# Gate projections inside an unrolled attention pipeline, and value products on 64 columns

## The chip, the core and the metric

One core of a Trainium2 chip. The time is the device time of one execution in microseconds (us); median of 3 runs before: 3261.18 (3258.07 to 3262.68). Engines: TensorE (PE: matmuls, and its weight loads, PEld), VectorE (DVE), ScalarE (ACT), GpSimd (POOL), SyncE (SP), which issues the DMAs.

## The reference

Two transformer blocks over one sequence of 512 tokens, 1024 wide, in float32. The change touches the mixer of the first:

```python
xn = rmsnorm(h, ln_mix_g[l])
z = xn @ w_in[l] + b_in[l]
q, k, v, pz, ga, gp = jnp.split(z, SPLITS, axis=-1)
y_a = sliding_window_attention(q, k, v, attn_sinks[l]) @ w_attn_up[l]
y_p = multiscale_pool(pz, w_pool_grp[l], pool_scale[l]) @ w_pool_up[l]
merged = jax.nn.sigmoid(ga) * y_a + jax.nn.sigmoid(gp) * y_p
h = h + merged @ w_o[l]
```

Attention has 16 query heads of 64 in two groups, each group with one key and value head. A block of 128 queries sees its own 128 keys and the 128 before them, and a sink value per head joins the softmax. The pool branch takes sliding means over 2, 4, 8 and 16 tokens. After this mixer come a product-key expert layer, a second mixer (RWKV and GLA scans) and a feed-forward layer; they make up most of the time.

## The kernel before

Activations lie with channels on the partitions: a tile is 128 channels by 512 tokens, and 1024 channels are 8 tiles.

**The weight stream.** All dense weights pass in one order through `Dense`, in slots of 128 x 1024 (512 KB), one for each output tile. To keep the precision of float32, a slot is split into a rounded high part and a low remainder: SP loads it raw (`load`, L141), ACT copies the high part (`high`, L150), POOL subtracts it for the low part (`low`, L158), and PE makes 24 matmuls of 512 columns of it, three for each of 8 input tiles (`product`, L256 to L258). Two slots can be raw and two split. `high` of a slot waits until PE has used the slot two before it (`used`), `low` waits for `high`, and a load waits for the split of the slot two before. Outputs go round over four PSUM banks, each given back (`free`) by the engine that reads it. Every engine has its own order of instructions, written out in the kernel, and waits for the others by semaphores.

**First mixer** (`first_mixer`), in three blocks with all engines joined between them:

1. *Projections*, 31 slots: 8 for queries, 8 for each of the two gates (sigmoid on the way out, L576), 4 for the pool input, 2 for keys, 1 for values. Values are wanted by token, so this slot's products take the activations as stationary operand: 96 matmuls of 128 columns, read out by DVE (L608).
2. *Attention* (`attention`), a loop over 4 blocks of 128 tokens. DVE first stages the block's queries and values (L829, L831). Then 8 steps of two heads each: score products (L792), DVE scales, masks and takes the maximum (L837 to L844), ACT exponentials (L873, L875), DVE normalises (L851 to L855), PE transposes (L805), ACT copies them (L882), PE value products (L816), ACT output (L886). PE issues the scores of two steps ahead between the transposes and the value products of a step. The value products of both heads add up in one output of 128 rows, with values padded with zeros in the half of the other head. POOL does the sliding sums of the pool branch meanwhile (L772 to L781). No weight slot is used in this block.
3. *Merge*, 20 slots: the pool groups' products (L722), 8 slots for the attention output, 4 for the pool branch, 8 for the output product. ACT first rounds the attention output (L383), then scales the four pool groups (L671), then makes high copies; DVE splits (L389, L691), then multiplies each result with its gate (L695, L699), which frees the bank.

Of the kernel before, what the change touches and what calls it, by code (L numbers as in the profile page):

```python
# [400 lines left out]
def layout_params(a):  # L401

    def col(v):
# [15 lines left out]
        ("b_v", np.broadcast_to(b[qw + kw:o_pool][None, :], (P, kw))),  # L419
# [38 lines left out]
def layout_constants():  # L458
# [22 lines left out]
    parts = [("mask", np.concatenate([mask0, mask, mask, mask], 1)), ("inv_count", inv), ("ident", ident),  # L481
# [27 lines left out]
def first_mixer(nc, k, dram):  # L509

    dense, norm, par, h, ps, consts = k.dense, k.norm, k.par, k.h, k.ps, k.consts
    with ExitStack() as ctx:
# [10 lines left out]
        vals = sb("values_by_token", [P, NB + 1, NKV * HD])  # L523
        yp = sb("pooled", [P, len(PW), T])
        cm = sb("mask_by_block", [P, NB, 2 * P])
# [4 lines left out]
        zeroed = sem("pool_engine_zeroed")  # L530
        x_in = [sem(f"x_loaded{n}") for n in range(4)]

        with nc.Block() as block:
            @block.sync
            def _(sp):
# [7 lines left out]
                sp.dma_start(cm[:, :, :], dram["consts"][:, 0:NB * 2 * P].rearrange("p (b n) -> p b n", b=NB)).then_inc(k.boot, 16)  # L543
                sp.dma_start(gw[:, :, :], dram["w_group"]).then_inc(k.boot, 16)
                w.run(sp, w.load, 7, BANK)
                w.run(sp, w.load, 1, 3)

            @block.gpsimd
            def _(pool):
                w = dense.cursor()  # L550
                pool.memset(keys[:, :, :, :], 0.0).then_inc(zeroed, 1)
                pool.memset(vals[:, 0, :], 0.0).then_inc(zeroed, 1)
                pool.memset(zp[:, :, 0:16], 0.0).then_inc(zeroed, 1)
                dense.low_first(pool)
                w.run(pool, w.low, 7, BANK)
                w.run(pool, w.low, 1, 3)

            @block.scalar
            def _(act):
# [21 lines left out]
                gemm_out(lambda m: ga[:, m, :], par("b_ga"), ACT.Sigmoid)  # L581
                gemm_out(lambda m: gp[:, m, :], par("b_gp"), ACT.Sigmoid)
# [27 lines left out]

            @block.tensor
            def _(pe):
# [4 lines left out]
                w.multiply(pe, 7, lambda t: chunk(xn, t), [DC], lambda t: norm.ready(pe, t))  # L617
                for v in range(NKV):
# [15 lines left out]
        dense.close(31, 32)  # L634
        ctx_xn.close()

        attention(nc, k, q, keys, vals, cm, zp, yp)
# [6 lines left out]
        group_done, group_out, group_split, rounded, split, merged, added = (sem(n) for n in (  # L644
            "pool_group_product", "pool_group_scaled", "pool_group_split", "merge_high", "merge_low", "gates_merged",
            "residual_added"))
        G = len(PW)
        with nc.Block() as block:
# [15 lines left out]
            def _(act):  # L664
# [20 lines left out]
            def _(dve):  # L685
# [11 lines left out]
                for m in range(DC):  # L697
                    dve.wait_ge(dense.used, w.slots + m // 2 + 1)
# [33 lines left out]
def attention(nc, k, q, keys, vals, masks, zp, yp):  # L732


    ps, par, consts = k.ps, k.par, k.consts
    with ExitStack() as ctx:
        def sb(name, shape, dt=F32):
# [4 lines left out]
        qs = sb("query_block", [P, QC, P])  # L742
        vs = sb("value_blocks", [P, 2, NKV, 2, P])
# [3 lines left out]
        mx, nm, su, es, den, rc = (sb(n, [P, NH]) for n in (  # L747
            "row_max", "negated_max", "row_sum", "sink_exp", "denominator", "reciprocal"))
        nsink = sb("negated_sinks", [P, NH])
        inv = sb("inverse_counts", [P, len(PW), T])  # L750
        w1, w2 = (sb(n, [P, len(PW), 16 + T]) for n in ("window_sums_a", "window_sums_b"))
        inv_in, zeroed, staged, scored, scaled, chain, negmax, exps, probs, turned, copied, mixed, out, pooled = (
            sem(n) for n in ("inverse_counts_loaded", "value_blocks_zeroed", "query_block_staged", "scores_product",
                             "scores_scaled", "attention_vector_chain", "negated_max_ready", "exps_done", "probs_ready",
                             "probs_transposed", "transposed_copied", "value_product", "attention_out", "pool_chain"))
        with nc.Block() as block:
            @block.sync
            def _(sp):
                sp.dma_start(inv[:, :, :], k.dram["inv_count"]).then_inc(inv_in, 16)
                sp.wait_ge(k.boot, 64)  # L760

            @block.gpsimd
            def _(pool):
                pool.memset(vs[:, :, :, :, :], 0.0).then_inc(zeroed, 1)
# [3 lines left out]
                src = zp  # L768
                for n, dst in enumerate((w1, w2, w1, w2)):
                    lag = PW[n] // 2  # L770
                    pool.wait_ge(pooled, 2 + n)
                    pool.tensor_tensor(dst[:, n:, 16:], src[:, n:, 16:], src[:, n:, 16 - lag:16 + T - lag],  # L772
                                       ALU.add).then_inc(pooled, 1)
                    src = dst
                pool.wait_ge(pooled, 6)
                pool.wait_ge(inv_in, 16)
                for g in range(len(PW)):
                    pool.tensor_tensor(yp[:, g, :], (w1, w2)[g % 2][:, g, 16:], inv[:, g, :], ALU.mult).then_inc(pooled, 1)
                for g in range(len(PW)):
                    pool.wait_ge(pooled, 7 + g)  # L780
                    pool.tensor_tensor(yp[:, g, :], yp[:, g, :], zp[:, g, 16:], ALU.subtract).then_inc(pooled, 1)  # L781

            @block.tensor
            def _(pe):
                with pe.Fori(0, NB) as b:
                    pe.wait_ge(staged, b * 3 + 3)

                    def scores(c):
                        if c >= 2:
                            pe.wait_ge(scaled, b * QC + (c - 1))  # L790
                        for half in range(2):
                            mm = pe.matmul(ps[:, c % 2, half * 2 * P:(half + 1) * 2 * P], qs[:, c, :],  # L792
                                           keys[:, c * NKV // QC, half, bass.ds(b * P, 2 * P)], start=True, stop=True)
                        mm.then_inc(scored, 1)

                    scores(0)
                    scores(1)
                    for c in range(QC):
                        pe.wait_ge(probs, b * QC + (c + 1))
                        if c:  # L800
                            pe.wait_ge(copied, b * QC + c)
                        for half in range(2):
                            for kb in range(2):
                                n = half * 2 + kb
                                mm = pe.transpose(ps[:, 2, n * P:(n + 1) * P], e[:, c % 2, half, kb * P:(kb + 1) * P],  # L805
# [2047 lines left out]
```

## Time and profile before

| | us |
|---|---|
| median of 3 runs | 3261.18 |
| profiled execution, its span (no other time of it is shown) | 3257.4 |
| PE busy | 2995.8 (92%) |
| DVE busy | 1793.6 (55%) |
| POOL busy | 1265.8 (39%) |
| ACT busy | 1068.2 (33%) |
| projections, from the first weight product to the value slot | 34.1 to 198.96 |
| attention block | 214.1 to 388.7 |

Busy times overlap between the engines. A PE record lasts longer than its share of PE's time, since matmuls are pipelined: the distance of starts counts.

### The profile page before, as it was taken

The numbers are of one execution on the slowest core, as the hardware profiler recorded it, in microseconds if no ns is written. First come the engines' busy times: TensorE is split into PE (matmuls) and PEld (weight loads), VectorE is DVE, ScalarE is ACT, GpSimd is POOL, SyncE is SP. The second block draws the span as 40 slices with busy tenths as digits, with TensorE's granted clock in tenths as the row PEclk, the third lists the DMA queues.
The fourth block names the chain that finished last, engine by engine and source line by source line (L and its number), as shares of the span: only waits on it lengthen the run. The fifth ranks groups of instructions, "written<-read, shape, count | busy, mean of one in ns | idle before, by whom it ended". The sixth has DMA issues, their size and how long they took to land. (4 is left out here: it accounts for less than half of the span.)

```text
span 3257.4 us, 52236 instructions
## 1 busy us (share of the span) xinstructions
PE 2995.8 (92%) x19808; PEld 2486.5 (76%) x19808; DVE 1793.6 (55%) x2626; ACT 1068.2 (33%) x1656; POOL 1265.8 (39%) x634
## 2 busy tenths in 40 slices
PE   7976698999999999999999999979869978899997
PEld 5864577888888888878888888856669966588775
DVE  1025426987477777427777777762836554433115
ACT  3324423333333333321111111134422335433323
POOL 3450033355444444444444444433332222244442
PEclk8988899999999999999999999989989989999998
DMA  3320022344445545565555555522652101233331
GB/s 119 97 71 0 7 85 90 92 141 141 126 163 205 175 159 174 211 185 190 197 196 196 196 190 190 184 91 78 205 150 52 36 15 39 65 96 96 98 104 65
DMA packets 173617, 404.59 MB, mean 124 GB/s; under 512 B 55216, under 2 KB 55344, under 8 KB 172208
## 3 DMA queue, kind: packets, MB, share of 16 engines
q1 hardware_dynamic: 173488, 402.72, 39.1%
q8 instruction: 100, 1.64, 0.2%
q14 instruction: 29, 0.24, 0.0%
HBM read 318.77 MB, written 83.89 MB: 124 GB/s over the span
## 5 line engine op out<-in xcount | busy, mean ns | idle before, releaser
L158 POOL TENSOR_TENSOR weights_low<-weights_raw,weights_high 128x1024 fp32r<-128x1024 f32 x435 | 1129.9, 2598 | 1686.6 <-ACT weights_high L150 1686.6
L150 ACT ACTIVATE weights_high<-weights_raw 128x1024 fp32r<-128x1024 f32 x435 | 461.0, 1060 | 1694.8 <-PE psum L258 1677.6
L256 PE MATMUL psum<-expert_in_high,weights_high 128*128 128x512 f32 x1152 | 458.4, 398 | 8.9 <-DVE expert_in_low L351 4.3
L257 PE MATMUL psum<-expert_in_low,weights_high 128*128 128x512 f32 x1152 | 449.7, 390 | 0.0
L258 PE MATMUL psum<-expert_in_high,weights_low 128*128 128x512 f32 x1152 | 449.6, 390 | 0.0
L256 PE MATMUL psum<-coefficients_high,weights_high 128*128 128x512 f32 x1024 | 399.6, 390 | 5.9 <-DVE coefficients_low L1172 4.2
L257 PE MATMUL psum<-coefficients_low,weights_high 128*128 128x512 f32 x1024 | 399.3, 390 | 0.0
L258 PE MATMUL psum<-coefficients_high,weights_low 128*128 128x512 f32 x1024 | 399.1, 390 | 0.0
L1172 DVE TENSOR_TENSOR coefficients_low<-activation_in,coefficients_high 128x512 fp32r<-128x512 f32 x128 | 354.8, 2772 | 4.4
L256 PEld LDWEIGHTS psum<-expert_in_high,weights_high 128*128 128x128 f32 x1152 | 217.1, 188 | 57.3 <-issue 10.2
L258 PEld LDWEIGHTS psum<-expert_in_high,weights_low 128*128 128x128 f32 x1152 | 216.8, 188 | 45.6
L257 PEld LDWEIGHTS psum<-expert_in_low,weights_high 128*128 128x128 f32 x1152 | 217.2, 189 | 41.3
L1153 DVE TENSOR_TENSOR second_key_weighted<-st_and_second_key_onehot,choices 128x512 f32<-128x512 f32 x128 | 225.7, 1763 | 19.4 <-DVE st_and_second_key_onehot L1149 2.2
L1169 DVE TENSOR_TENSOR coefficients_high<-activation_in,table_group 128x512 fp32r<-128x512 f32 x128 | 88.6, 692 | 264.6 <-PE psum L258 264.6
L256 PEld LDWEIGHTS psum<-coefficients_high,weights_high 128*128 128x128 f32 x1024 | 192.8, 188 | 46.7 <-DVE coefficients_low L1172 4.6
L258 PEld LDWEIGHTS psum<-coefficients_high,weights_low 128*128 128x128 f32 x1024 | 192.8, 188 | 40.2
L257 PEld LDWEIGHTS psum<-coefficients_low,weights_high 128*128 128x128 f32 x1024 | 192.8, 188 | 40.1
L1149 DVE TENSOR_TENSOR st_and_second_key_onehot<-tables,choices 128x1024 f32<-128x1024 f32 x128 | 157.1, 1227 | 115.1 <-PE psum L1050 100.5
L256 PE MATMUL psum<-mix_in_high,weights_high 128*128 128x512 f32 x464 | 187.3, 404 | 33.4 <-POOL weights_low L113 14.8
L257 PE MATMUL psum<-mix_in_low,weights_high 128*128 128x512 f32 x464 | 182.4, 393 | 0.0
L258 PE MATMUL psum<-mix_in_high,weights_low 128*128 128x512 f32 x464 | 182.2, 393 | 0.0
L256 PE MATMUL psum<-ffn_in_high,weights_high 128*128 128x512 f32 x352 | 138.3, 393 | 4.8 <-DVE ffn_in_low L351 4.8
(390 smaller groups left out, 4786.1 us busy)
## 6 DMA issues: line engine op xcount, KB each, us to landing
weights_raw<-in_weights SPq DMA_DIRECT2D x437, 512.0 KB, 3.6
expert_activations<-expert_activation SPq DMA_DIRECT2D x128, 256.0 KB, 4.2
coefficient_table<-table_stage SPq DMA_DIRECT2D x8, 4096.0 KB, 13.6
table_group<-coefficient_table SPq DMA_DIRECT2D x128, 256.0 KB, 4.1
activation_in<-expert_activations SPq DMA_DIRECT2D x128, 256.0 KB, 3.7
chunk_vectors<-scan_vectors SPq DMA_DIRECT2D x8, 1280.0 KB, 8.4
scan_vectors<-scan_stage SPq DMA_DIRECT2D x4, 1280.0 KB, 6.7
scan_vectors<-scan_stage SPq DMA_DIRECT2D x4, 1024.0 KB, 6.0
```

Of the source, the lines that this page charges most:

```text
L150: act.activation(d.hi[:, m % SPLIT, :], d.raw[:, m % RAW, :], ACT.Copy).then_inc(d.high, 1)
L158: pool.tensor_tensor(d.lo[:, m % SPLIT, :], d.raw[:, m % RAW, :], d.hi[:, m % SPLIT, :].bitcast(F32), ALU.subtract).then_inc(d.split, 1)
L256: pe.matmul(acc, w[0][:, cols], x[0], start=start, stop=False)
L257: pe.matmul(acc, w[0][:, cols], x[1], start=False, stop=False)
L258: return pe.matmul(acc, w[1][:, cols], x[0], start=False, stop=stop)
L1149: dve.tensor_tensor(onehot[:, u, :, :, :], iota[:, None, None, :].to_broadcast([P, 2, QT, NK]), sel[:, 0:2, bass.ds(t, QT)][:, :, :, None] ...
L1153: dve.tensor_tensor(second[:, u, :, :], onehot[:, u, 1, :, :], sel[:, 2, bass.ds(t, QT)][:, :, None].to_broadcast([P, QT, NK]), ALU.mult). ...
L1169: dve.tensor_tensor(by_block(co[0][:, o, :]), by_block(tile), gt, ALU.mult).then_inc(ex.part, 1)
L1172: dve.tensor_tensor(co[1][:, o, :], tile, co[0][:, o, :].bitcast(F32), ALU.subtract).then_inc(ex.coef, 1)
```

## The change

The gates' 16 slots move from the projections into the attention block, and with them their place in the weight stream. The loop over blocks is unrolled into 32 steps. In each, PE does 12 of the gates' 24 matmuls per slot between the scores of two steps ahead and the value products; ACT reads the gates out after each second step, without the sigmoid, which ACT applies in the merge. Queries, keys and values are no longer staged per block. The value slot has the usual form; its result by channel is transposed by PE and copied by DVE twice, once for each half. Attention's banks are 4 to 7. The value products of each head have 64 columns of the array and 64 output rows, in turn by head.

Core of the diff ("..." where lines are left out; DVE's and the score products' lines in attention change in their indices only, `q` and `keys` being read in place):

```diff
-        vals = sb("values_by_token", [P, NB + 1, NKV * HD])
+        vals = sb("values_by_token", [P, NB + 1, NKV, 2, P])
...
-                w.run(sp, w.load, 7, BANK)
+                w.run(sp, w.load, 3, BANK)
...
                 gemm_out(lambda m: q[:, m, :], par("b_q"), ACT.Identity)
-                gemm_out(lambda m: ga[:, m, :], par("b_ga"), ACT.Sigmoid)
-                gemm_out(lambda m: gp[:, m, :], par("b_gp"), ACT.Sigmoid)
...
                 w.high(act, 0, NKV, 3)
+                w.full_wait(act, 0, NKV)
+                act.activation(vt[:, :], dense.acc[NKV], ACT.Identity, bias=par("b_v")).then_inc(dense.free[NKV], 1)
                 act.sem_inc(dense.free[3], 1)
...
-                w = dense.cursor()
-                w.advance(7 * BANK)
-                w.full_wait(dve, 0, 2)
-                dve.tensor_tensor(vals[:, 1:, :], dense.acc[2].rearrange("p (b n) -> p b n", b=NB),
-                                  par("b_v")[:, None, :].to_broadcast([P, NB, P]), ALU.add).then_inc(dense.free[2], 1)
+                dve.wait_ge(zeroed, 3)
+                dve.wait_ge(turned, 1)
+                for half in range(2):
+                    dve.tensor_copy(vals[:, 1:, :, half, half * HD:(half + 1) * HD],
+                                    ps[:, 5, :].rearrange("p (b v n) -> p b v n", b=NB, v=NKV))
...
-                w.multiply(pe, 7, lambda t: chunk(xn, t), [DC], lambda t: norm.ready(pe, t))
-                for v in range(NKV):
+                w.multiply(pe, 3, lambda t: chunk(xn, t), [DC], lambda t: norm.ready(pe, t))
+                for v in range(NKV + 1):
...
-                w.free_wait(pe, 0, 2)
-                w.slot_wait(pe, 0, 2, 3)
-                wv = w.weights(2)
+                pe.wait_ge(dense.free[NKV], w.units // BANK + 2)
                 for b in range(NB):
-                    cols = slice(b * P, (b + 1) * P)
-                    for t in range(DC):
-                        x, y = chunk(xn, t, cols), (wv[0][:, t * P:(t + 1) * P], wv[1][:, t * P:(t + 1) * P])
-                        mm = product(pe, dense.acc[2][:, cols], x, 0, y, t == 0, t == DC - 1)
-                mm.then_inc(dense.used, 1)
+                    mm = pe.transpose(ps[:, 5, b * P:(b + 1) * P], vt[:, b * P:(b + 1) * P], consts("ident"))
+                mm.then_inc(turned, 1)
         norm.close(squares=DC, roots=1, splits=1)
...
-                for g in range(G):
-                    act.wait_ge(group_done, g + 1)
-                    for dst in (yps, ypp[0]):
-                        ins = act.activation(dst[:, g, :], ps[:, 4 + g, :], ACT.Copy, scale=par("pool_scale")[:, g:g + 1])
-                    ins.then_inc(group_out, 1)
-                w.run(act, w.high, 2, BANK)
+
+                def gate(x, m):
+                    act.activation(x[:, m, :], x[:, m, :], ACT.Sigmoid).then_inc(gated, 1)
+
+                for m in range(DC):
+                    gate(ga, m)
+                for j in range(DC):
+                    w.high(act, 0, j, DC)
+                    if j < G:
+                        act.wait_ge(group_done, j + 1)
+                        for dst in (yps, ypp[0]):
+                            ins = act.activation(dst[:, j, :], ps[:, 4 + j, :], ACT.Copy, scale=par("pool_scale")[:, j:j + 1])
+                        ins.then_inc(group_out, 1)
+                    gate(gp, j)
+                w.advance(DC)
...
+                    dve.wait_ge(gated, m + 1)
...
+    STEPS, GATES = NB * QC, 2 * DC
+    PART = DC * GATES // STEPS
+    TURNED, OUT = 6, 7
...
+        inv = gp[:, 0:len(PW), :]
...
+                w = dense.cursor()
+                for j in range(GATES):
+                    w.load(sp, 0, j, GATES)
...
+                w.low(pool, 0, 0, GATES)
...
+                w.low(pool, 0, 1, GATES)
...
+                for j in range(2, GATES):
+                    w.low(pool, 0, j, GATES)
...
+                def gate_part(n):
+                    j, first = n * PART // DC, n * PART % DC
+                    if first == 0:
+                        w.free_wait(pe, j // BANK, j % BANK)
+                        w.slot_wait(pe, 0, j, GATES)
+                    for t in range(first, first + PART):
+                        mm = product(pe, dense.acc[j % BANK], w.weights(j), t, chunk(xn, t), t == 0, t == DC - 1)
+                    if first + PART == DC:
+                        mm.then_inc(dense.used, 1)
+
+                scores(0)
+                scores(1)
+                for n in range(STEPS):
+                    b, kv = n // QC, n % QC * NKV // QC
+                    pe.wait_ge(probs, n + 1)
+                    if n:
+                        pe.wait_ge(copied, n)
+                    for half in range(2):
+                        for kb in range(2):
+                            at = half * 2 + kb
+                            mm = pe.transpose(ps[:, TURNED, at * P:(at + 1) * P], e[:, n % 2, half, kb * P:(kb + 1) * P],
+                                              consts("ident"))
+                    mm.then_inc(turned, 1)
+                    if n + 2 < STEPS:
+                        scores(n + 2)
+                    gate_part(n)
+                    pe.wait_ge(copied, n + 1)
+                    if n:
+                        pe.wait_ge(out, n)
...
+                    for kb in range(2):
                         for half in range(2):
+                            at = half * 2 + kb
+                            mm = pe.matmul(ps[rows(half), OUT, 0:P], vals[:, b + kb, kv, half, rows(half)],
+                                           pt[:, at * P:(at + 1) * P], start=(kb == 0), stop=(kb == 1))
+                    mm.then_inc(mixed, 1)
...
+                def gate_out(j):
+                    dst, bias = (ga, par("b_ga")) if j < DC else (gp, par("b_gp"))
+                    if j == DC:
+                        act.wait_ge(pooled, 6 + len(PW))
+                    w.high(act, 0, j, GATES)
+                    w.full_wait(act, j // BANK, j % BANK)
+                    act.activation(dst[:, j % DC, :], dense.acc[j % BANK], ACT.Identity,
+                                   bias=bias[:, j % DC:j % DC + 1]).then_inc(dense.free[j % BANK], 1)
+
+                exp(0)
+                exp(1)
+                for n in range(STEPS):
+                    act.wait_ge(turned, n + 1)
+                    act.activation(pt[:, :], ps[:, TURNED, :], ACT.Copy).then_inc(copied, 1)
+                    if n + 2 < STEPS:
+                        exp(n + 2)
+                    if (n + 1) * PART % DC == 0:
+                        gate_out((n + 1) * PART // DC - 1)
+                    act.wait_ge(mixed, n + 1)
+                    act.activation(q[:, n % QC, block_of(n)], ps[:, OUT, 0:P], ACT.Copy).then_inc(out, 1)
+        dense.close(GATES, GATES)
...
-    w_z = np.concatenate([w_in[:, 0:qw], w_in[:, o_ga:], w_in[:, o_pool:o_ga], wk[0], wk[0], wk[1], wk[1],
-                          w_in[:, qw + kw:o_pool]], 1)
+    w_z = np.concatenate([w_in[:, 0:qw], w_in[:, o_pool:o_ga], wk[0], wk[0], wk[1], wk[1], w_in[:, qw + kw:o_pool],
+                          w_in[:, o_ga:]], 1)
```

## Rows read from the trace of the kernel before

**Rows 1.** The page: PE's line of busy time, and the clock in 40 slices.

```profile
PE 2995.8 (92%) x19808; PEld 2486.5 (76%) x19808; DVE 1793.6 (55%) x2626; ACT 1068.2 (33%) x1656; POOL 1265.8 (39%) x634
...
PEclk8988899999999999999999999989989989999998
```

**Rows 2.** Stretches: us, busy (instructions) by engine, clock, DMA share, GB/s; projections, attention.

```profile
34.10:198.96 164.86, 164.86 (x720) 136.28 (x719) 0.00 (x0) 53.47 (x63) 71.09 (x30) 0.99 0.32 101
...
214.10:388.70 174.60, 103.41 (x512) 82.92 (x512) 92.42 (x205) 77.11 (x260) 22.04 (x15) 0.80 0.03 9
```

**Rows 3.** Instructions of L576: duration min/median/max ns, first and last start.

```profile
L576 ACT ACTIVATE q_then_attention_out<-psum,params x8: 668/668/668, 42.4 to 80.5; 128x512 f32 x8
...
L576 ACT ACTIVATE gate_pool<-psum,params x8: 668/668/668, 129.4 to 167.5; 128x512 f32 x8
L576 ACT ACT_TABLE_LOAD  x2: 1283/1283/1283, 86.0 to 107.8; - x2
```

**Rows 4.** Timeline, value slot to attention: start, duration, engine, line, operation, [idle before].

```profile
198.96 0.22 PE L256 MATMUL psum<-weights_high,mix_in_high 128*128 128x128 f32 x1
...
209.83 0.69 DVE L608 TENSOR_TENSOR values_by_token<-psum,params 128x512 f32<-128x512 f32 x1 [179.08 <-PE psum L258]
...
211.02 2.34 POOL L158 TENSOR_TENSOR weights_low<-weights_raw,weights_high 128x1024 fp32r<-128x1024 f32 x1 [8.29 <-ACT weights_high L150]
...
214.12 0.33 SPq L759 DMA_DIRECT2D inverse_counts<-in_consts  x1
```

**Rows 5.** Timeline, the start of attention.

```profile
215.94 3.89 DVE L831 COPY value_blocks<-values_by_token 128x256 f32 x2
...
219.98 3.78 PE L792 MATMUL psum<-keys_by_kv_and_half,query_block 128*128 x8 [10.19 <-DVE value_blocks L831]
...
228.92 1.11 PE L805 MATMUL psum<-tables,probabilities 128*128 128x128 f32 x4 [5.16 <-DVE probabilities L855]
```

**Rows 6.** Timeline, a settled attention step.

```profile
245.22 0.66 PE L805 MATMUL psum<-tables,probabilities 128*128 128x128 f32 x4 [1.75 <-DVE probabilities L855]
...
245.72 1.03 PE L792 MATMUL psum<-keys_by_kv_and_half,query_block 128*128 x4
...
246.58 1.14 PE L816 MATMUL psum<-probabilities_transposed,value_blocks 128*128 128x128 f32 x8
246.78 0.69 DVE L837 SCALAR_TENSOR_TENSOR scores<-psum,mask_by_block 128x512 f32<-128x512 f32 x1 [1.62 <-PE psum L792]
...
248.42 0.51 ACT L873 ACTIVATE probabilities<-scores,negated_max 128x256 f32<-128x256 f32 x1 [1.91 <-DVE negated_max L844]
...
248.72 0.69 DVE L855 TENSOR_TENSOR probabilities<-probabilities,reciprocal 128x512 f32<-128x512 f32 x1
...
249.47 0.66 PE L805 MATMUL psum<-tables,probabilities 128*128 128x128 f32 x4 [1.74 <-DVE probabilities L855]
```

**Rows 7.** Timeline, DVE with POOL at work beside it.

```profile
231.17 5.39 POOL L781 TENSOR_TENSOR pooled<-pooled,pool_in 128x512 f32<-128x512 f32 x4
...
231.78 0.69 DVE L837 SCALAR_TENSOR_TENSOR scores<-psum,mask_by_block 128x512 f32<-128x512 f32 x1 [2.92 <-PE psum L792]
...
233.99 1.45 DVE L855 TENSOR_TENSOR probabilities<-probabilities,reciprocal 128x512 f32<-128x512 f32 x1
```

**Rows 8.** Timeline of PE in the second mixer's scan: 32 small records.

```profile
2504.63 1.15 PE L2007 MATMUL psum<-X_transposed,L_level_times_X 64*64 64x64 f32 x32
```

**Rows 9.** Timeline, the start of the merge.

```profile
388.78 4.27 ACT L383 ACTIVATE ion_out_then_merged_high<-q_then_attention_out 128x512 fp32r<-128x512 f32 x8 [0.54 <-PEq L756]
...
397.70 0.69 DVE L691 TENSOR_TENSOR pool_groups_split_low<-pool_in,pool_groups_split_high 128x512 fp32r<-128x512 f32 x1 [0.47 <-ACT pool_groups_split_high L671]
...
403.44 1.06 ACT L150 ACTIVATE weights_high<-weights_raw 128x1024 fp32r<-128x1024 f32 x1 [4.38 <-PE psum L258]
```

**Rows 10.** Timeline, PE's first matmul after an idle gap.

```profile
463.45 0.76 PE L256 MATMUL psum<-ion_out_then_merged_high,weights_high 128*128 128x512 f32 x1 [5.65 <-DVE tion_out_then_merged_low L389]
```

**Rows 11.** The stretch behind that gap, columns as in rows 2.

```profile
464.00:468.00 4.00, 4.00 (x11) 3.03 (x10) 4.00 (x7) 2.28 (x4) 0.00 (x0) 0.50 0.04 15
```

More of the change, by code:

```diff
@@ L551, in _ @@
                 pool.memset(keys[:, :, :, :], 0.0).then_inc(zeroed, 1)
-                pool.memset(vals[:, 0, :], 0.0).then_inc(zeroed, 1)
+                pool.memset(vals[:, :, :, :, :], 0.0).then_inc(zeroed, 1)
                 pool.memset(zp[:, :, 0:16], 0.0).then_inc(zeroed, 1)
                 dense.low_first(pool)
-                w.run(pool, w.low, 7, BANK)
+                w.run(pool, w.low, 3, BANK)
                 w.run(pool, w.low, 1, 3)
@@ L697, in _ @@
                 for m in range(DC):
+                    dve.wait_ge(gated, DC + m + 1)
                     dve.wait_ge(dense.used, w.slots + m // 2 + 1)
@@ L746, in attention, with score_bank, rows, block_of @@
         pt = sb("probabilities_transposed", [P, 4 * P])
-        mx, nm, su, es, den, rc = (sb(n, [P, NH]) for n in (
+        mx, nm, su, es, den, rc = (sb(n, [P, 2 * STEPS]) for n in (
             "row_max", "negated_max", "row_sum", "sink_exp", "denominator", "reciprocal"))
         nsink = sb("negated_sinks", [P, NH])
[L750 to L755, printed above, removed]
+        inv = gp[:, 0:len(PW), :]
+        w1, w2 = (sb(n, [P, len(PW) - at, 16 + T]) for at, n in enumerate(("window_sums_a", "window_sums_b")))
+        inv_in, scored, scaled, chain, negmax, exps, probs, turned, copied, mixed, out, pooled = (
+            sem(n) for n in ("inverse_counts_loaded", "scores_product", "scores_scaled", "attention_vector_chain",
+                             "negated_max_ready", "exps_done", "probs_ready", "probs_transposed", "transposed_copied",
+                             "value_product", "attention_out", "pool_chain"))
+        def score_bank(n):
+            return ps[:, 4 + n % 2, :]
+        def rows(half):
+            return slice(half * HD, (half + 1) * HD)
+        def block_of(n):
+            return slice(n // QC * P, (n // QC + 1) * P)
         with nc.Block() as block:
@@ L781, in _ @@
                     pool.tensor_tensor(yp[:, g, :], yp[:, g, :], zp[:, g, 16:], ALU.subtract).then_inc(pooled, 1)
+                for j in range(2, GATES):
+                    w.low(pool, 0, j, GATES)
             @block.tensor
             def _(pe):
[L785 to L790, printed above, removed]
-                        for half in range(2):
[L792 to L805, printed above, removed]
-                                                  consts("ident"))
-                        mm.then_inc(turned, 1)
-                        if c + 2 < QC:
-                            scores(c + 2)
-                        pe.wait_ge(copied, b * QC + (c + 1))
-                        if c:
-                            pe.wait_ge(out, b * QC + c)
-                        for half in range(2):
-                            for kb in range(2):
-                                n = half * 2 + kb
-                                mm = pe.matmul(ps[:, 3, 0:P], vs[:, kb, c * NKV // QC, half, :], pt[:, n * P:(n + 1) * P],
-                                               start=(n == 0), stop=(n == 3))
-                        mm.then_inc(mixed, 1)
-                    pe.wait_ge(out, b * QC + QC)
@@ new lines, in _, with scores @@
+                w = dense.cursor()
+                def scores(n):
+                    c = n % QC
+                    if n >= 2:
+                        pe.wait_ge(scaled, n - 1)
+                    for half in range(2):
+                        mm = pe.matmul(score_bank(n)[:, half * 2 * P:(half + 1) * 2 * P], q[:, c, block_of(n)],
+                                       keys[:, c * NKV // QC, half, n // QC * P:n // QC * P + 2 * P], start=True, stop=True)
+                    mm.then_inc(scored, 1)
@@ new lines, in _, with scale_and_max @@
+                link = Count(chain, 1)
+                def scale_and_max(n):
+                    r, h = slice(2 * n, 2 * n + 2), slice(n % QC * 2, n % QC * 2 + 2)
+                    dve.wait_ge(scored, n + 1)
+                    dve.scalar_tensor_tensor(
+                        out=s[:, n % 2, :, :], in0=score_bank(n).rearrange("p (g n) -> p g n", g=2), scalar=SCALE,
+                        in1=masks[:, int(n >= QC):int(n >= QC) + 1, :].to_broadcast([P, 2, 2 * P]),
+                        op0=ALU.mult, op1=ALU.add).then_inc(scaled, 1)
+                    dve.wait_ge(scaled, n + 1)
+                    link.inc(dve.tensor_reduce(mx[:, r], s[:, n % 2, :, :], AXX, ALU.max))
+                    link.wait(dve)
+                    dve.scalar_tensor_tensor(out=nm[:, r], in0=mx[:, r], scalar=-1.0, in1=nsink[:, h],
+                                             op0=ALU.mult, op1=ALU.min).then_inc(negmax, 1)
@@ new lines, in normalise @@
+                def normalise(n):
+                    r = slice(2 * n, 2 * n + 2)
+                    dve.wait_ge(exps, 4 * (n + 1))
+                    link.inc(dve.tensor_tensor(den[:, r], su[:, r], es[:, r], ALU.add))
+                    link.wait(dve)
+                    link.inc(dve.reciprocal(rc[:, r], den[:, r]))
+                    link.wait(dve)
+                    dve.tensor_tensor(e[:, n % 2, :, :], e[:, n % 2, :, :],
+                                      rc[:, r, None].to_broadcast([P, 2, 2 * P]), ALU.mult).then_inc(probs, 1)
@@ new lines, in _, with exp @@
+                w = dense.cursor()
+                def exp(n):
+                    act.wait_ge(negmax, n + 1)
+                    for half in range(2):
+                        j, head = 2 * n + half, n % QC * 2 + half
+                        act.activation(e[:, n % 2, half, :], s[:, n % 2, half, :], ACT.Exp, bias=nm[:, j:j + 1],
+                                       accum_out=su[:, j:j + 1]).then_inc(exps, 1)
+                        act.activation(es[:, j:j + 1], par("sinks")[:, head:head + 1], ACT.Exp,
+                                       bias=nm[:, j:j + 1]).then_inc(exps, 1)
```

98 lines of the change are left out of this document (25 added, 73 removed).

## The prediction

> **What bounds the kernel now.** I read the page first. TensorE (PE) is busy 92% of the span, and the granted clock is lower than elsewhere in the first slice and in slices 3 to 5, 163 to 407 us [rows 1]. The change touches only the first mixer, so I cut that into stages. The input projection is a solid block of PE work: 164.86 us busy out of 164.86 at clock 0.99. The attention is not: in 174.60 us PE is busy 103.41, VectorE (DVE) 92.42, ScalarE (ACT) 77.11, nothing is loaded, and the clock averages 0.80 [rows 2]. So the first stage is bound by PE, the second by a chain of small steps.
>
> That chain is one attention step (two heads of one block), 32 in all. In a settled step the transposes start at 245.22 and the next ones at 249.47: 4.25 us. In between PE issues transposes (0.50 us to the start of the scores), scores (0.86 to the start of the value products) and value products; DVE takes the scores at 246.78 and ends the normalising multiply at 248.72 + 0.69 = 249.41; the transposes follow [rows 6]. The eight value records have 128 moving columns each and the four score records 256, 1,024 in both, so the value products take the same 0.86 to issue. PE therefore works 0.50 + 0.86 + 0.86 = 2.22 us of 4.25 and waits for DVE in the rest. Four blocks have 8 x 4.25 = 34 us of this each, 136 in all; the other 38 us are starts and ends of blocks, where the clock is low.
>
> **Part 1, the projection loses 16 weight slots.** The last query output starts at 80.5 and the last gate output, 16 slots later, at 167.5: 87.0 us, 5.44 a slot [rows 3]. ACT's, GpSimd's (POOL) and SP's share of these slots lies beside PE, so exactly PE's time goes: -87.0.
>
> The value slot changes form. Before, its 96 short matmuls run from 198.96 to 209.8 [rows 4]; now it has 24 matmuls of 512 columns like every slot, 5.44: -5.4. Its end gets longer. Before, the last split (0.2 handoff, 1.06 high, then low until 213.36) ended the stage and attention began at 214.12, 4.3 after PE. Now, behind the same high copy, come one 0.67 activation, four transposes (0.66), two DVE copies of 512 elements (0.69 each, taking the price of a row that reads as much), four handoffs of about 0.1, then the same 0.7 for the change of block: 5.1, so +0.8. If DVE's copies are held up by POOL's split it is 0.7 more. Sum: -91.6; attention starts at about 122.5.
>
> **Part 2, the start of attention.** Staging of queries and values is gone; it held the first scores until 219.98, mostly two DVE copies of 3.89 us behind POOL's window sums [rows 5]. That is 5.9 us after 214.12; now 0.3. From first scores to first transposes it is 8.9 us, at half clock with the window sums alongside; this stays. First transposes: 122.5 + 0.3 + 8.9 = 131.7.
>
> **Part 3, the loop.** Each step gets 12 of the gates' matmuls, half a slot: 2.72. They stand behind the scores of two steps ahead and in front of the value products. The DVE chain starts at the scores, so it is not lengthened: probabilities are ready 4.25 after the step's start as before. PE's own work becomes 2.22 + 2.72 = 4.94, more than 4.25. PE becomes the bound, with 0.7 us of margin per step for everybody else. I checked the others by laying an odd step (the one that ends a slot) out from 0, with these durations: exponentials 3.2 to 4.65, gates' last matmul done 4.4, high copy 4.65 to 5.7, gate output to 6.4, attention output of this step to 6.65, transposed copy of the next step to 7.3; the value products of the next step are issued at 9.0. ACT has 1.7 to spare. POOL's low split (2.4) runs 5.75 to 8.15; SP's loads of 512 KB fit many times over. The next slot's weights are needed only three steps later.
>
> The value products: four matmuls of 64 columns of the array, in alternation between the halves. Moving columns are as many as before. Bounds: the scans' products on a quarter of the array with 64 moving columns issue 32 records in 1.15 us, tail included, some 29 ns each [rows 8]. At the pace of the score records (0.86 / 1,024 columns) a record of 64 columns takes 54, so there two quarters run side by side. Those differ in rows and in columns, our halves in columns only. If ours ran side by side, a step would lose 0.43: 4.51. On the other side a record of 128 columns lasts 0.27 us and more against 0.11 of issue, so a pipe emptied at a seam costs about 0.17; at four seams a step that is 0.68: 5.62. I take 5.1, near the plain count, with one seam.
>
> The Trainium skill (TensorEngine Tiling (Array Packing), Key Properties) says that changing the tiling mode drains TensorE. No row here goes between the 64-column and the full form in a dense stretch, so the trace doesn't decide it; by the rule there are two such changes per step, 0.34, and the step would be 5.28, 6 us more in all. The skill (TensorE: Matmul & The Clock Gate, Part 3, What overlaps and what doesn't) also has weight loads overlap only where the row group differs, which speaks against the gain of 0.43; the scan's rows fit it, as their halves do differ in rows.
>
> 32 x 5.1 = 163.2. The last two steps issue no scores: -1.7. At the start the clock is at half: after an idle spell it was for 4.8 us of dense work [rows 10, 11], which loses 2.4. In the first steps POOL also has window products and differences to do: with POOL at work a DVE multiply of two SBUF operands took 1.45 rather than 0.69, the scaling that reads PSUM stayed at 0.69 [rows 7]; this lengthens some five chains by about 1, of which the margin takes 0.7: +1. Sum 164.9; PE ends at 296.6. The block then ends not with PE but with the last split for the merge: the gates' last matmul is about 0.6 before PE's end, then high 1.06, low 2.4, 0.7 for the block: 300.2. Before: 388.8. So -88.6 to here; attention itself takes 177.7 against 174.6.
>
> **Part 4, the merge gets the sigmoids.** ACT rounds eight tiles in 4.27 [rows 9], then loads a table (1.28, [rows 3]) and does eight sigmoids at 0.67: 10.9 after the merge's start. Only then comes the high copy that slot 2 needs; with the low copy it is done at 14.4, just when PE has used slots 0 and 1 (ACT took slot 1's release at 403.44, 14.7 after the start). No loss. But the pool groups' output number j is now behind the high copy of slot j, which waits until slot j was used, and DVE multiplies no gate before it has split all four groups. Group 3: slot 3 used at 25.5, high to 26.6, two activations to 27.9, split 28.6, product 29.3. PE needs that bank for unit 4 at 25.3: +4.1. Before, the groups were split by 398.4, in slot 1.
>
> Two idle gaps are new: 3.5 us ahead of the merge and these 4.1. After a gap of 5.65 PE ran at half clock for 4.8 [rows 10, 11], a loss of 2.4; I take half of that for each gap, +2.4. Sum of the merge: +6.5.
>
> **Sum.** -91.6 + 3.1 + 6.5 = -82.0. Nothing later is edited. The profiled execution shows only its span, 3257.4; with the change 3175.4. The median of the runs shown is 3.8 above that span, and I carry this over: 3261.2 - 82.0 = 3179.
>
> **Rivals.**
> (a) POOL takes DVE's place in the loop. Each slot's low split (2.4) could fall on the normalising multiply, which then waits for it [rows 7]. For: 16 splits are new here. Against: by the layout they fall in the even step's PSUM-reading scaling, and end before its multiply. Price: 4.25 + 2.4 = 6.65 in one step of two instead of 5.1: 16 x 1.55 = +25, 3204.
> (b) Better than forecast: halves side by side, and no loss of clock in the merge: 32 x 0.59 = 19 less, but never under the chain's 4.25: 3158 to 3165.
> (c) The chains don't overlap: a wait puts the gates' matmuls between scores and DVE or delays the transposes by them, and a step is 4.25 + 2.72 = 6.97. +60: 3239. Against: scores stand ahead of the gates on PE, and their semaphore is on the score product itself.
> (d) Slower than before: the clock stays at half in the mixed loop. A step then is 9.9, +154, 3333. It decides against the change from (5.1 + 82 / 32 =) 7.7 us per step, that is, with the clock at half in over half of the loop. For: attention's average of 0.80. Against: the low clock there goes with idle starts of blocks, and steps in which PE was idle for 1.7 of 4.25 us ran at full clock [rows 6]; now PE never pauses. The skill's TensorE page (Part 4) says that transposes don't count as busy in the same way; here they are a tenth of PE's time, and no row isolates it.
>
> **Chances.** Forecast 0.72 (3162 to 3200: step 4.6 to 5.6, merge +3 to +10), (a) 0.12, (b) 0.09, (c) 0.04, (d) 0.03. A measurement of this kernel tells about 0.2%, 6.5 us, from no change; only (d) and unforeseen losses end there or beyond it: faster 0.95, same 0.01, slower 0.04. Range 3162 to 3205.
>
> **What would show it.** Right: projection ends near 118, first transposes near 132, 32 steps of 5.0 to 5.2 in which PE waits for nothing, merge from about 300, one PE wait of 4 us on DVE's gate product after slot 3. Wrong: PE waiting for the multiply in the loop (a), value products at half their issue time (b), steps near 7 (c), granted clock 0.5 after the first steps (d).

## The result and the profile after

| | before | after |
|---|---|---|
| median, us | 3260.64 (4 runs) | 3169.96 (4 runs, 3168.03 to 3171.49) |
| ratio | | 0.9718, 95% interval 0.9704 to 0.9732 |
| span of the profiled execution | 3257.4 | 3166.7 |

The change saves 90.7 us; 82 were forecast, and the time lies in the range given (3162 to 3205). In the page of the kernel after, PE's line and the clock [rows 1] read:

```profile
PE 2960.5 (93%) x19740; PEld 2449.9 (77%) x19740; DVE 1794.3 (57%) x2615; ACT 1066.7 (34%) x1666; POOL 1265.6 (40%) x633
...
PEclk9999999999999999999999999989899988999998
```

The dip of the clock in slices 3 to 5 is gone. The kernel's stretches (columns as [rows 2]) are the projections, the start of attention, and the loop from its second step to just before its end:

```profile
34.10:112.00 77.90, 77.90 (x341) 64.33 (x340) 0.00 (x0) 23.04 (x29) 32.03 (x14) 0.99 0.33 108
...
120.50:129.87 9.37, 2.92 (x8) 1.89 (x9) 7.95 (x10) 2.93 (x12) 8.98 (x6) 0.55 0.48 168
...
137.00:284.00 147.00, 145.99 (x855) 114.08 (x852) 78.04 (x177) 88.83 (x266) 46.86 (x23) 1.00 0.17 54
```

PE is busy 145.99 of 147.00 us in the loop; in the attention block before it was busy 103.41 of 174.60 [rows 2]. The timeline of one step, against [rows 6], with the gates' matmuls left out:

```profile
137.15 0.66 PE L840 MATMUL psum<-tables,probabilities 128*128 128x128 f32 x4
...
137.64 1.03 PE L816 MATMUL psum<-keys_by_kv_and_half,q_then_attention_out 128*128 128x256 f32 x4
...
138.71 0.69 DVE L865 SCALAR_TENSOR_TENSOR scores<-psum,mask_first_and_other 128x512 f32<-128x512 f32 x1 [3.38 <-PE psum L816]
...
140.62 0.69 DVE L882 TENSOR_TENSOR probabilities<-probabilities,reciprocal 128x512 f32<-128x512 f32 x1
...
141.36 0.66 PE L852 MATMUL psum<-probabilities_transposed,values_by_token 128*64 128x128 f32 x8
...
141.95 0.66 PE L840 MATMUL psum<-tables,probabilities 128*128 128x128 f32 x4
```

The probabilities are ready at 140.62 + 0.69 = 141.31; PE comes for them at 141.95 and doesn't wait. The step is 4.79 (4.79 to 4.81 in 27 of the 31 distances between transposes; the first, at half clock, is 7.28), and the value products take 0.59 of it. The merge is where time was given back. Its first instructions, PE's wait after slot 3, and the stretch behind that wait:

```profile
288.86 4.28 ACT L383 ACTIVATE ion_out_then_merged_high<-q_then_attention_out 128x512 fp32r<-128x512 f32 x8 [2.46 <-PEq L774]
288.88 5.28 PE L729 MATMUL psum<-pooled,pool_group_weights 128*128 128x512 f32 x8 [3.79 <-PEq L774]
...
318.31 1.78 DVE L696 TENSOR_TENSOR pool_groups_split_low<-pool_in,pool_groups_split_high 128x512 fp32r<-128x512 f32 x1 [3.59 <-ACT pool_groups_split_high L675]
320.01 2.47 DVE L701 TENSOR_TENSOR gate_attention<-psum,gate_attention 128x512 f32<-128x512 f32 x4
```

```profile
320.93 0.76 PE L256 MATMUL psum<-ion_out_then_merged_high,weights_high 128*128 128x512 f32 x1 [4.97 <-DVE gate_attention L701]
```

```profile
320.93:326.19 5.26, 5.26 (x13) 4.09 (x13) 1.55 (x3) 0.00 (x0) 0.00 (x0) 0.50 0.23 93
```

In the kernel before, the pool groups' products, the first row of PE in the merge, ran at full clock:

```profile
388.80 3.67 PE L722 MATMUL psum<-pooled,pool_group_weights 128*128 128x512 f32 x8 [0.96 <-PEq L756]
```

| mark in the timeline, us | before | forecast | after |
|---|---|---|---|
| attention starts | 214.1 | 122.5 | 120.6 |
| first transposes | 228.9 | 131.7 | 129.9 |
| a settled step | 4.25 | 5.1 | 4.79 |
| merge starts | 388.8 | 300.2 | 288.9 |
| first product with the expert keys, after the merge | 535.5 | 453.5 | 445.0 |

The lead is 99.9 us at the merge's start and 90.5 behind it.

### The profile page after: what moved, and what is told of

The parts are those of the page before. It is cut to its first block and busy times, and to the rows that moved or that the text cites. A ratio compares the mean times of both kernels' runs of the same rounds, so it can differ in the third digit from the quotient of the medians.

```text
span 3166.7 us, 51665 instructions
## 1 busy us (share of the span) xinstructions
PE 2960.5 (93%) x19740; PEld 2449.9 (77%) x19740; DVE 1794.3 (57%) x2615; ACT 1066.7 (34%) x1666; POOL 1265.6 (40%) x633
## 5 line engine op out<-in xcount | busy, mean ns | idle before, releaser
L256 PE MATMUL psum<-mix_in_high,weights_high 128*128 128x512 f32 x472 | 196.3, 416 | 33.2 <-POOL weights_low L113 14.8
```

The source lines that it names most:

```text
L256: pe.matmul(acc, w[0][:, cols], x[0], start=start, stop=False)
```

## The experiments

All times but one are medians of several executions, measured beside the kernel before, whose own median was 3258.3 to 3262.8 on these occasions. A step is the distance from one step's transposes to the next one's; a settled step is one away from the start and the end of the loop.

**Where the 91 us come from.** The first leaves the unrolled attention and puts the gates back in the projections, with the sigmoid there and the merge as before; the loop keeps everything but the gates' matmuls, with their loads, splits and read-outs:

```diff
-                    gate_part(n)
```

> One part alone: the unrolled attention, the new value slot and the 64-column products, but the gates' 16 slots back in the projections with their sigmoid, and the merge as before. Theory (the gain is mostly the overlap): attention is 9.3 to its first transposes and 32 x 4.25 from there, some 146 in place of 174.7; projections 4.5 less than before; merge as before: 3260.6 - 29 - 4.5 = 3227. So 57 of the 91 us come from the overlap. Rival (unrolling and the staging that goes make most of it): 3200 or less.

3249.7, ratio 0.9971 (0.9958 to 0.9983): neither figure holds, and it is 23 us worse than my own, which had steps of 4.25. The steps go 4.22, 4.85, 5.52, 4.98, 5.52, and so on. Two stretches in the loop of that kernel have the reason in the clock column:

```profile
240.00:260.00 20.00, 13.83 (x63) 9.07 (x61) 9.08 (x23) 7.40 (x26) 0.00 (x0) 0.61 0.00 0
280.00:300.00 20.00, 13.27 (x64) 8.80 (x64) 9.21 (x24) 8.19 (x30) 0.00 (x0) 0.67 0.00 0
```

In this loop the granted clock is at full or at half by turns, and these are its means. So I took the same kernel with value products on all 128 columns:

```diff
-                    for kb in range(2):
-                        for half in range(2):
+                    for half in range(2):
+                        for kb in range(2):
                             at = half * 2 + kb
-                            mm = pe.matmul(ps[rows(half), OUT, 0:P], vals[:, b + kb, kv, half, rows(half)],
-                                           pt[:, at * P:(at + 1) * P], start=(kb == 0), stop=(kb == 1))
+                            mm = pe.matmul(ps[:, OUT, 0:P], vals[:, b + kb, kv, half, :],
+                                           pt[:, at * P:(at + 1) * P], start=(at == 0), stop=(at == 3))
```

> As the run with the gates back in the projections (3249.7, steps of 4.8 to 5.5 at a clock of 0.66 on average where 4.25 was expected), but the value products on the full 128 columns. Theory (the 64-column form leaves PE so little work that the granted clock falls again and again): steps of 4.25 at clock 1.00 as in the kernel before, attention 148 instead of 166.6, 3231. Rival (the unrolled loop itself lets the clock fall): 3249 to 3255.

3226.0, ratio 0.9899 (0.9883 to 0.9916). All settled steps are 4.22, the clock column is 1.00:

```profile
280.00:300.00 20.00, 12.51 (x80) 10.19 (x80) 11.34 (x27) 10.69 (x40) 0.00 (x0) 1.00 0.00 0
```

Without the gates' matmuls in the loop the 64-column form costs 24 us. This run also divides the 91 us. Unrolling with the new value slot brings some 33 (3259.4 to 3226.0): attention starts at 208.1 instead of 214.1 and lasts 145.4 instead of 174.7, and the distances of 12.1 to 12.2 between blocks are gone. The gates' matmuls in the loop bring some 51 more, net of what the merge gives back (3226.0 to 3174.7, the changed kernel with full columns, below), and the 64-column form some 5.

Why does the form cost time here? Is it the form, or PE's smaller amount of work? The version with the gates in the projections again, each group of value products made twice:

```diff
+                    for _ in range(2):
```

> The version with the gates back in the projections and 64-column value products (3249.7), each group of value products made twice into the same place. Theory (it is PE's share of work in a step that keeps the clock): PE has as much array time as with full columns (0.86), the clock stays at full, steps of 4.22, 3226, though work was added. Rival (64-column products don't keep the clock up whatever their number): clock near 0.66 as before, steps 4.5 to 5.5, 3250 or more.

3226.1, clock 1.00, all settled steps 4.22. Twice the products, 23.6 us faster: it is not the form.

```profile
280.00:300.00 20.00, 12.73 (x120) 9.62 (x120) 11.36 (x28) 10.09 (x37) 0.00 (x0) 1.00 0.00 1
```

Doubling the products does two things, though: PE works more in each step, and its pause before the transposes is shorter, 1.68 us instead of 2.11 in a step of 4.22. These runs don't separate the two; the run with the gates ahead of the scores, below, says a little more.

The other way round, the 64-column form alone in the kernel before, in its loop:

> The kernel before with one edit alone: its value products on 64 columns each, loop and all else kept. Theory (with nothing else for PE to do, the quicker products let the granted clock fall in steps that ran at full clock): the settled steps alternate between 4.22 and 5.5, a mean near 5.0; some 26 of 32 steps are settled, +0.75 each: +15 to +20, 3275 to 3280, slower than before. Rival (the clock fell in the unrolled version for another reason): steps stay 4.25 since the vector chain sets them, 3260.

3273.8, ratio 1.0036 (1.0023 to 1.0049), slower by some 12. Settled steps are 4.7 to 5.55 mostly, a few 4.25; I had expected 15 to 20. The rival, steps that stay at 4.25, falls.

**The 64 columns inside the mixed loop.** The changed kernel with full columns, by the edit of the value products shown above:

> The changed kernel with the value products back on the full 128 columns (zero-padded values, one sum over both heads), all else kept. Theory (halves of the array work side by side): the eight value records take 0.86 us to issue again instead of 0.43, and the two seams around the 64-column form (0.13 before, 0.17 behind) go, so a settled step is 4.94 instead of 4.79: 32 x 0.15 = +5, 3175; if seams of 0.3 remain, +14, 3184. Rival (the 64-column form is of no account): step 4.79, 3170.

3174.7, ratio 0.9739 (0.9722 to 0.9755), step 4.93. The theory's 4.94 holds; the form brings 0.14 a step there, 4.5 us. Then the changed kernel in another order, head 0 first, then head 1:

```diff
-                    for kb in range(2):
-                        for half in range(2):
+                    for half in range(2):
+                        for kb in range(2):
```

> The changed kernel with the value products in the order head 0, head 0, head 1, head 1 instead of in turn. Theory (neighbouring matmuls run side by side where they sit on different columns, in order of issue): only the middle pair overlaps, three times 0.21 instead of two: +0.21 a step, 5.00, +7, 3177. Rival 1 (order is of no account, the array sorts them): 4.79, 3170. Rival 2 (the 64-column form is quick for another reason than working side by side): 4.79 as well, so e1 has to tell these apart.

3172.0, step 4.81: the theory's 5.00 falls, and both rivals' 4.79 holds. Order is of no account, but this left open why. So I timed the products by themselves, behind the loop of the changed kernel and a warm-up of 16 full products; each group is

```diff
+                for i in range(8):
+                    pe.matmul(ps[lo, 4, :], vals[:, 1 + i % 4, 0, 0, lo], q[:, i, :], start=True, stop=True)
```

with these forms: full columns (L861: 128 moving columns, L865: 512), one half alone (L863: 128, L867: 512), halves in turn (L869: 512), full and half in turn (L875, L873: 128). Each product leaves two records in the trace.

> The disputed cost by itself: behind the attention loop of the changed kernel, groups of eight float32 products whose results nobody uses, after sixteen of 512 moving columns as a warm-up. Theory (halves side by side): 64 columns of one half alone take as long as the full 128 columns (128 moving: 0.11 us a record; 512: 0.21 a record, 0.43 a product), and only in turn between the halves half of that. Rival 1 (a product of at most 64 columns streams one moving column a cycle instead of one in two): half the time already on one half alone, at 128, 256 and 512 moving columns. Rival 2 (the weight load sets the pace at 128 moving columns): half the time at 128 moving columns, no gain at 512. Full and half form in turn: a seam of 0.15 each time, or none.

The time of this kernel (3207.0, one execution) says nothing; the timeline of PE in that stretch does:

```profile
301.07 1.95 PE L861 MATMUL psum<-q_then_attention_out,values_by_token 128*128 128x128 f32 x16
302.94 1.96 PE L863 MATMUL psum<-q_then_attention_out,values_by_token 128*64 128x128 f32 x16
304.83 7.13 PE L865 MATMUL psum<-q_then_attention_out,values_by_token 128*128 128x512 f32 x16
311.90 6.65 PE L867 MATMUL psum<-q_then_attention_out,values_by_token 128*64 128x512 f32 x15
317.96 0.64 PE L869 MATMUL psum<-q_then_attention_out,values_by_token 128*64 128x512 f32 x1
318.39 0.59 PE L867 MATMUL psum<-q_then_attention_out,values_by_token 128*64 128x512 f32 x1
318.44 3.97 PE L869 MATMUL psum<-q_then_attention_out,values_by_token 128*64 128x512 f32 x15
322.34 0.49 PE L875 MATMUL psum<-q_then_attention_out,values_by_token 128*128 128x128 f32 x2
322.76 0.43 PE L873 MATMUL psum<-q_then_attention_out,values_by_token 128*64 128x128 f32 x2
323.12 0.49 PE L875 MATMUL psum<-q_then_attention_out,values_by_token 128*128 128x128 f32 x2
```

One half alone is no faster than the full array: 1.89 us for 16 records against 1.87, some 0.43 a record against 0.44 at 512 moving columns, and 0.22 for both at 256. Halves in turn take (322.34 - 318.44) / 15 = 0.26, the change of form behind them included: side by side, and both rivals fall. (My figure of 0.21 for one record of 512 was a slip; it is 0.43, and a product has two.) The fifth and sixth row explain the order: a record of L869 starts at 317.96, before the last record of L867 (318.39), which stands ahead of it in the program. L869's first product is for the half on which L867 still works, so I take the early record for its second product, on the free half; the row doesn't name the half. Read so, a free half takes the next product queued for it, and each half works off its own. Two records of each form in turn take 323.12 - 322.34 = 0.78. Within a group such records start 0.11 apart ((1.95 - 0.27) / 15 for L861), so 0.44 is work, and two changes of form (seams) cost 0.17 each.

**The place of the gates.** The changed kernel with the gates' matmuls ahead of the scores:

```diff
                     mm.then_inc(turned, 1)
+                    gate_part(n)
                     if n + 2 < STEPS:
                         scores(n + 2)
-                    gate_part(n)
```

> The changed kernel with the gates' 12 matmuls ahead of the scores of two steps ahead instead of behind them. Theory (the vector chain that starts at the scores runs beside the gates' matmuls, and that alone hides them): the chain and the matmuls add up, step 4.25 + 2.72 = 6.97, +70, 3240, about the kernel before. Rival (PE has the same work and is the bound in any order): step 4.8 to 5.0, 3170 to 3176.

3241.3, ratio 0.9946; the step is 6.96 to 6.98 in 24 of the 31 distances, and 8.14 to 8.56 in five, at half clock or with POOL's pool work alongside. PE waits 2.11 in a settled step for the multiply:

```profile
207.93 0.66 PE L840 MATMUL psum<-tables,probabilities 128*128 128x128 f32 x4 [2.11 <-DVE probabilities L882]
```

The same work on every engine, 71 us apart by one place in PE's order. This run also bears on the question left open above. Its pause of 2.11 is that of the 64-column loop without the gates, but with more work beside it, and over 80 us of it the clock is 1.00:

```profile
185.00:265.00 80.00, 54.79 (x316) 42.23 (x317) 28.95 (x72) 33.77 (x105) 11.97 (x5) 1.00 0.11 34
```

So a pause of that length doesn't bring the clock down each time by itself. It did fall in three other steps of this run, so the amount of work is the likelier cause in the loop without the gates, and isn't proven.

**What the merge gives back.** ScalarE's order there, with VectorE's waits set to match:

```diff
-                for m in range(DC):
-                    gate(ga, m)
-                for j in range(DC):
-                    w.high(act, 0, j, DC)
-                    if j < G:
-                        act.wait_ge(group_done, j + 1)
+                for j in range(G):
+                    act.wait_ge(group_done, j + 1)
...
+                gate(ga, 0)
+                for j in range(DC):
+                    w.high(act, 0, j, DC)
+                    if j + 1 < DC:
+                        gate(ga, j + 1)
                     gate(gp, j)
```

> The changed kernel, in the merge ScalarE gives out the four pool groups before the first high copy, and one attention gate's sigmoid behind each high copy instead of all eight ahead. Theory (the merge loses time because VectorE's first gate product stands behind group 3, and that behind the use of slot 3): PE's stall of 5.0 us after slot 3 goes, and the half clock behind it (4.8 us of dense work at half, 2.4): -7.4, 3162.6. Rival (the sigmoids as such are too much for ScalarE there): another wait takes its place on PE, -2 at most.

3163.2, ratio 0.9704 (0.9688 to 0.9720), 6.8 less than the changed kernel, as the theory has it; PE's wait for the gate product is gone and none takes its place. The kernel before took 1.3 less beside this run and the next two than beside the changed kernel, so their gains may be that much smaller.

**The idle start of attention.** The first slot of the gates goes in front of the first transposes, and ScalarE reads the gates out accordingly:

```diff
                 scores(1)
+                gate_part(0)
+                gate_part(1)
...
-                    gate_part(n)
+                    if n + 2 < STEPS:
+                        gate_part(n + 2)
```

> The changed kernel, with the first slot of the gates multiplied between the first two score products and the first transposes, where PE idles 6.3 us, and each later part two steps earlier; the last two steps have no gates. Theory: two parts of 2.72 leave the loop (-5.4, +1 for waits of the last steps), the first step runs at full clock (-2.5) but starts 1.3 later, the last split no longer ends the block (-2.7) and the merge starts at full clock (-1.6): -10, 3160. Rival (the start of attention is bound by the clock, not by idle time): the parts only move, 0 to -3.

3160.1, ratio 0.9692 (0.9676 to 0.9709): -9.9, the theory's 10. Then both edits together:

> Both edits of the two runs before together. If they touch different gaps they add: -17, 3153. If the merge's clock loss is shared between them: -15.

3154.0, ratio 0.9678 (0.9662 to 0.9694): -16.0 against a sum of -16.7: the two add. This version beats both kernels. Its start of attention, against the second stretch of the kernel after:

```profile
120.50:129.80 9.30, 8.68 (x29) 7.05 (x30) 6.90 (x11) 2.93 (x12) 8.47 (x5) 0.72 0.46 171
```

## Why the prediction was right, and where it was off

- **Projections** (-91.6 forecast): -93.5 at the start of attention. PE's last record ends at 116.2, and attention starts 4.3 behind it, as before the change; the forecast had 5.1. The first product also began 0.7 earlier than in the profile before (32.7 against 33.5), which no edit explains. These two make 1.5 of the 1.9, so the slots' 87.0 and the value slot held.
- **Start of attention**: 9.3 to the first transposes, 9.2 forecast.
- **PE becomes the bound, the DVE chain stays at 4.25**: shown by PE's missing wait in the timeline and by the run with the gates ahead of the scores, whose 6.97 is the sum of both parts. POOL's low split fell where the layout had it: in the even step, 5.7 after the odd one's start. Rival (a) happens only in the first steps, when POOL has its pool work as well: there two multiplies in the loop took 1.47 us instead of 0.69, and two distances are 5.15 and 5.58, together 1.2 over. From then on every multiply took 0.69.
- **The step's size is the term that was off**: 5.1 forecast, 4.79 measured, 32 x 0.31 = 9.9 us. I weighed halves side by side (-0.43) against seams (+0.17 each), and took one seam and no gain. Both are real: the products by themselves show halves side by side and seams of 0.17, and the 0.14 between the forms in the loop is 0.43 to 0.44 gained and 0.3 lost at two seams. The bounds of 4.51 and 5.62 held the result. The Trainium skill (TensorEngine Tiling (Array Packing), Key Properties) has a drain at each change of mode; the seam of 0.17 agrees. My second sentence from the Trainium skill (TensorE: Matmul & The Clock Gate, Part 3, What overlaps and what doesn't), that weight loads overlap only where the row group differs, was read as speaking against the gain; here halves with the same rows work side by side, and the measurement decides.
- **The merge was under-sized**: +6.5 forecast, 9.4 measured. The stall was 5.0 instead of 4.1, as DVE's last group split waited 1.1 for POOL's low split (1.78 instead of 0.69), an effect I had counted in the loop but not here. And both idle gaps were followed by half clock, where I had counted half of that: the group products at the merge's start took 5.28 instead of 3.67, 1.6 more, and behind the stall PE worked 5.26 us at a clock of 0.50, a loss of 2.6. 5.0 + 1.6 + 2.6 are 9.2 of the 9.4.
- **Rival (b)** came true by half: the halves do work side by side, but with two seams, and the merge did lose clock. So the time is neither in its 3158 to 3165 nor at my 3179, but between them.
- **Rival (c)** is what the run with the gates ahead of the scores built, at 6.97 as priced. **Rival (d)** did not occur; but a clock that falls in this loop is real: it costs 24 us once the gates' matmuls are out and the value products have 64 columns.

The mechanism was right: the gates' matmuls hide in the chain, and PE becomes the bound. The sum missed by 8.7 us, with errors of -9.9 in the step, -1.9 in the projections and +2.9 in the merge. Only the last went against the others, so little of the hit is luck; but the sign of 32 steps of 5.0 to 5.2 didn't come true, and the choice of one seam was a guess between two bounds.

## What to carry to other kernels

Dense matmuls hide in a latency chain if they stand right behind the product that starts the chain, on an engine whose own work then sets the pace; ahead of it they add in full. Before a product in such a chain is made cheaper, look at the granted clock: in the loop without the gates the cheaper products cost 24 us. When work moves to another engine's ordered queue, follow what that queue now gives out later, here the pool groups' output behind a copy that waits for a slot.

## What was not expected of the hardware

- Less PE work made attention slower: with 64-column value products and no gates in the loop the granted clock went back and forth between its two levels (1.2 and 2.4 GHz; 0.61 and 0.67 on average in the stretches shown), and steps took up to 5.52 instead of 4.22. Doing the products twice brought both back. Whether the work or the shorter pause does it was not fully separated.
- Column halves of the array seem to take products out of program order: a record started 0.43 us before one that stands ahead of it. The Trainium skill (TensorE: Matmul & The Clock Gate, Part 3, What overlaps and what doesn't) says that matmuls start strictly in program order; this trace differs.
- A change between full and 64-column form costs about 0.17 us by itself, and two of them about 0.3 in the loop.
